# A transformer layer on one core: the lower left output quadrant is added on VectorE and stored plainly

## What is computed

```python
    mix = jnp.concatenate([attn_out, u], axis=-1) @ w_out[l]
    x = x + g1 * mix                                    # called x1 below
    h2 = modulate(rms_norm(x, norm_ffn_w[l]), sh2, sc2)
    up = depthwise_conv(h2 @ w_up[l], ffn_conv_w[l], ffn_conv_b[l])
    gate, val = jnp.split(up, 2, axis=-1)
    x = x + g2 * ((jax.nn.silu(gate) * val) @ w_down[l])   # (1024 x 2816) @ (2816 x 1024)
```

## Time and profile before

| | |
|---|---|
| median of 3 runs | 1184.42 us (1182.46 to 1187.9) |
| profiled execution | 1190.29 us, of which the span from the first to the last instruction is 1188.4 us |
| mean granted TensorE clock | 0.983 |
| busy share of the span | PE 95%, DVE 79%, ACT 49%, POOL 25% |
| DMA | 171.77 MB, 145 GB/s in the mean |

### The profile page before, as it was taken

The page is one execution under the profiler, slowest core; times in us unless marked ns, Lnnn a source line. Parts: engine busy times, 40 slices in busy tenths (PEclk is TensorE's granted clock), DMA queues, the critical chain, the costliest instruction groups (busy, mean ns, idle before and its releaser), DMA issues.

```text
span 1188.4 us, 17094 instructions
## 1 busy us (share of the span) xinstructions
PE 1128.5 (95%) x5953; PEld 959.4 (81%) x5953; DVE 937.2 (79%) x1422; ACT 577.2 (49%) x991; POOL 296.4 (25%) x337
## 2 busy tenths in 40 slices
PE   7899999899998999998799999999999999999995
PEld 7687888799888887876688888787888878888884
DVE  0579988779997754469999999999999966877763
ACT  1662356766556764455343434343443534444441
POOL 2200111135454000002555454545510020000111
PEclk9999999999998999999899999999999999999998
DMA  9422556529999315222545454545433284543574
GB/s 364 159 75 77 120 107 117 145 46 257 245 240 277 107 46 170 86 88 90 159 127 180 135 171 131 171 129 175 136 111 106 91 307 159 118 114 98 125 160 62
DMA packets 103090, 171.77 MB, mean 145 GB/s; under 512 B 9322, under 2 KB 62690, under 8 KB 102004
## 3 DMA queue, kind: packets, MB, share of 16 engines
q1 hardware_dynamic: 82388, 104.70, 26.7%
q0 software_dynamic: 20640, 66.27, 23.9%
HBM read 112.21 MB, written 31.46 MB: 121 GB/s over the span
## 4 chain that ended last, share of the span: by engine, by line
PE 37%; DVE 13%; issue 7%; ACT 5%; DVEq 0%; ACTq 0%; POOL 0%
PE ps L1684 14%; PE ps L1734 6%; PE ps L1736 6%; PE ps L1735 6%; PE ps L1649 5%; DVE y L2100 3%; DVE w_op L2001 3%; DVE w_raw L2019 2%; DVE y L2096 2%; ACT w_op L1805 2%; ACT y L1893 1%; DVE u L2089 1%; DVE s_sum L2019 1%; ACT h_second L1798 0%; PE ps L1660 0%
## 5 line engine op out<-in xcount | busy, mean ns | idle before, releaser
L1684 PE MATMUL ps<-t_op,w_op 128*128 128x512 f32 x1056 | 247.5, 390 | 2.5 <-issue 0.9
L1684 PEld LDWEIGHTS ps<-t_op,w_op 128*128 128x128 f32 x1056 | 197.9, 188 | 46.0 <-issue 2.9
L1684 PE MATMUL ps<-hx,w_op 128*128 128x512 f32 x792 | 192.0, 396 | 9.6 <-DVE u L2089 7.0
L1684 PEld LDWEIGHTS ps<-hx,w_op 128*128 128x128 f32 x792 | 151.0, 191 | 43.3 <-DVE u L2089 6.5
L1805 ACT ACTIVATE w_op<-w_raw 128x512 fp32r<-128x512 f32 x132 | 79.9, 623 | 193.8 <-DVE w_raw L2019 191.6
L1734 PE MATMUL ps<-dnh,ah 128*128 128x512 f32 x308 | 120.1, 390 | 1.6 <-DVE dnl L2107 1.6
L1735 PE MATMUL ps<-dnl,ah 128*128 128x512 f32 x308 | 119.8, 389 | 0.0
L1736 PE MATMUL ps<-dnh,al 128*128 128x512 f32 x308 | 119.8, 389 | 0.0
L2001 DVE TENSOR_TENSOR w_op<-w_raw,w_op 128x512 fp32r<-128x512 f32 x132 | 102.5, 791 | 9.8 <-ACT w_op L1805 7.7
L1913 ACT ACTIVATE ah<-hid 128x512 fp32r<-128x512 f32 x77 | 48.6, 631 | 116.8 <-PE ps L1736 112.8
L2107 DVE TENSOR_TENSOR al<-hid,ah 128x512 fp32r<-128x512 f32 x77 | 53.3, 692 | 48.8 <-ACT ah L1913 48.1
(11 more groups left out here) (293 smaller groups left out, 2392.2 us busy)
## 6 DMA issues: line engine op xcount, KB each, us to landing
w_raw<-in_w_up SPq DMA_DIRECT2D x44, 512.0 KB, 5.1
wm<-in_w_mod SPq DMA_DIRECT2D x32, 512.0 KB, 6.4
sums<-wm POOLq DMA_DIRECT2D x32, 512.0 KB, 8.1
wd<-in_w_down POOLq DMA_DIRECT2D x44, 256.0 KB, 3.4
w_down_sums<-wd POOLq DMA_DIRECT2D x44, 256.0 KB, 2.8
dn_raw<-w_down_sums SPq DMA_DIRECT2D x44, 256.0 KB, 2.6
hid_scratch<-hid SPq DMA_DIRECT2D x20, 512.0 KB, 4.4
hid<-hid_scratch POOLq DMA_DIRECT2D x20, 512.0 KB, 5.2
```

The lines of the kernel that those rows point to most:

```text
L1684: last = pe.matmul(bank_of(p, s), w_op[p][w][:, k, :], rows_of(p, k, v), start=(start and k == 0 and w == 0 and v == 0), stop=(k == KH - 1 ...
```

## The change

It touches only the lower left quadrant.

- GpSimd's 4 adding transfers of `w21` and 4 of `c21` are gone, with the wait between them. GpSimd's last wait is now for the 12 transfers that are left, of which those of c12 are the last.
- Before the load of step 49 (`BASE_STEP = (7, 5)`: product 7, pair 5) SP issues 4 loads of the lower left quadrant of x1 (256 KB each) from `out` into `p1_all`. Ahead of them it waits for the x1 stores and for the last `u2`.
- New quad operation `b21` behind each `c12`: VectorE adds `w21` to the loaded x1 in `p1_all`.
- At the end `c21` writes its product with the gate into `w21`, and a new quad operation `o21` adds it to `p1_all`: one more VectorE operation per row block.
- SP then waits for each `o21`, stores `p1_all` to `out` without adding (256 KB each, 4 of them), and waits for the four stores.

```diff
-        QUAD_OPS += [(name, t) for t in range(4) for name in ("s12", "c12")] + [("c21", t) for t in range(4)]
+        QUAD_OPS += [(name, t) for t in range(4) for name in ("s12", "c12", "b21")] + [(name, t) for t in range(4) for name in ("c21", "o21")]
+        BASE_STEP = (7, 5)
...
+            def lower_left(t):
+                return out[0, HALF + t * P:HALF + (t + 1) * P, 0:HALF]
...
                 for n in range(4, NSTEP):
+                    if n == step_of(*BASE_STEP):
+                        sp.wait_ge(x1_out, 16 * TT)
+                        sp.wait_ge(quad_read, quad_at("u2", 3))
+                        for t in range(TT // 2):
+                            sp.dma_start(p1_all[:, t, :], lower_left(t)).then_inc(base_in, 16)
                     load_step(n)
+                for t in range(TT // 2):
+                    sp.wait_ge(quad_read, quad_at("o21", t))
+                    sp.dma_start(lower_left(t), p1_all[:, t, :]).then_inc(x1_out, 16)
+                sp.wait_ge(x1_out, 16 * (TT + TT // 2))
...
+                    elif name == "b21":
+                        dve.wait_ge(base_in, 16 * (TT // 2))
+                        ins = dve.tensor_tensor(out=p1_all[:, t, :], in0=p1_all[:, t, :], in1=w21[:, t, :], op=ALU.add)
+                    elif name == "c21":
+                        dve.wait_ge(bank_mm, TT // 2 - 1 + t + 1)
+                        ins = dve.tensor_tensor(out=w21[:, t, :], in0=ps[:, t, :], in1=g2[0], op=ALU.mult)
                     else:
-                        dve.wait_ge(bank_mm, TT // 2 - 1 + t + 1)
-                        ins = dve.tensor_tensor(out=p1_all[:, t, :], in0=ps[:, t, :], in1=g2[0], op=ALU.mult)
+                        ins = dve.tensor_tensor(out=p1_all[:, t, :], in0=p1_all[:, t, :], in1=w21[:, t, :], op=ALU.add)
...
                 for t in range(TT // 2):
                     quad("c21", t)
+                    quad("o21", t)
...
-                    accumulate("c22", t, 1, 1, g22[:, t, :], stored)
-                    accumulate("w21", t, 1, 0, w21[:, t, :], w21_stored)
+                    accumulate("c22", t, 1, 1, g22[:, t, :])
                 for t in range(TT // 2):
-                    accumulate("c12", t, 0, 1, g12[:, t, :], stored)
-                pool.wait_ge(w21_stored, 16 * 4)
-                for t in range(TT // 2):
-                    accumulate("c21", t, 1, 0, p1_all[:, t, :], stored)
-                pool.wait_ge(stored, 16 * 16)
+                    accumulate("c12", t, 0, 1, g12[:, t, :])
+                pool.wait_ge(stored, 16 * 12)
```

More of the change, by code:

```diff
@@ L1501, in build @@
             back_in = [sem4(f"back_in{i}") for i in range(NXT)]
-            dn_sum, dn_hi, dn_split, dn_mm, bank_mm, p1_copied, quad_read, stored, w21_stored = (
-                sem4(n) for n in ("dn_sum", "dn_hi", "dn_split", "dn_mm", "bank_mm", "p1_copied", "quad_read", "stored", "w21_stored"))
+            dn_sum, dn_hi, dn_split, dn_mm, bank_mm, p1_copied, quad_read, stored, base_in = (
+                sem4(n) for n in ("dn_sum", "dn_hi", "dn_split", "dn_mm", "bank_mm", "p1_copied", "quad_read", "stored", "base_in"))
             block = s4.enter_context(nc.Block())
@@ L2227, in _ @@
                     if i in (1, 3, 5, 7):
-                        for name in {6: ("c11",), 5: ("u2",), 7: ("u4",), 3: ("s22", "c22", "w21"), 4: ("s12", "c12")}.get(p, ()):
+                        for name in {6: ("c11",), 5: ("u2",), 7: ("u4",), 3: ("s22", "c22", "w21"), 4: ("s12", "c12", "b21")}.get(p, ()):
                             quad(name, i // 2)
@@ L2274, in _, with accumulate @@
                     reload(i)
-                def accumulate(name, t, rows_half, cols_half, src, done):
+                def accumulate(name, t, rows_half, cols_half, src):
                     pool.wait_ge(quad_read, quad_at(name, t))
                     r0 = (rows_half * (TT // 2) + t) * P
-                    pool.dma_start(out[0, r0:r0 + P, cols_half * HALF:(cols_half + 1) * HALF], src, accum_op=ALU.add).then_inc(done, 16)
+                    pool.dma_start(out[0, r0:r0 + P, cols_half * HALF:(cols_half + 1) * HALF], src, accum_op=ALU.add).then_inc(stored, 16)
                 pool.wait_ge(x1_out, 16 * TT)
                 for t in range(TT // 2):
-                    accumulate("c11", t, 0, 0, g11[:, t, :], stored)
+                    accumulate("c11", t, 0, 0, g11[:, t, :])
                 for t in range(TT // 2):
-                    accumulate("c22", t, 1, 1, g22[:, t, :], stored)
-                    accumulate("w21", t, 1, 0, w21[:, t, :], w21_stored)
+                    accumulate("c22", t, 1, 1, g22[:, t, :])
                 for t in range(TT // 2):
-                    accumulate("c12", t, 0, 1, g12[:, t, :], stored)
-                pool.wait_ge(w21_stored, 16 * 4)
-                for t in range(TT // 2):
-                    accumulate("c21", t, 1, 0, p1_all[:, t, :], stored)
-                pool.wait_ge(stored, 16 * 16)
+                    accumulate("c12", t, 0, 1, g12[:, t, :])
+                pool.wait_ge(stored, 16 * 12)
 def rope_table(np):
```

## The result

The changed kernel takes 1178.91 us in the median of 12 runs (1174.95 to 1186.06), the kernel before beside it 1186.59 (1181.91 to 1193.35, 12 runs). The ratio is 0.9941 with a 95% interval of [0.9913, 0.9968]: 7.0 us faster. The prediction had 7.2 us (1177.2 from 1184.42).

A forecast was written before the change was run, and what follows sets the result against it. TensorE, busy 95% of the span, was taken as the bound, leaving mainly the end to gain: VectorE +0.95, issue -0.63, landing -3.0, DRAIN -4.5, together -7.2 us from 1184.42 to 1177.2 us; range 1173.5 to 1183.5.

The forecast's parts named there:

- What bounds: Whole kernel: TensorE is busy 95% of the span; other engines' savings show only where it stands still, chiefly the last 12.1 us.
- VectorE, +0.95: End of the kernel: the last VectorE operation ends 0.95 us later, 0.72 for o21 and 3 x 0.08 for the pace.
- the part of the pace: Last four row blocks: dependent c21 and o21 pairs take 1.44 us against 1.36 per row block, costing 3 x 0.08 us.
- VectorE to issue, -0.63: End of the kernel: SP issues the last store 0.03 us after VectorE, where GpSimd's adding transfer took 0.66.
- Landing, -3.0: Last store: SP's plain store lands in 2.6 us (bounds 2.5 to 3.6) instead of 5.6 for the adding transfer.
- The DRAIN, -4.5: Block end: GpSimd's DRAIN of 4.63 us is hidden under the last product's matmuls; SP's of 0.12 us comes last instead.
- The rival in which it stays last: Block end: GpSimd's DRAIN still ends last or SP gets a costly one; only -2.7 us, 1181.7 us; chance 0.08.
- The loads, no cost: Before step 49: four issues of 0.32 us fit between loads; step 49's data lands in 5 to 6 us, under 9.4.
- TensorE's second cover of 3.5 us: Step 49: after ScalarE takes the load, another 3.5 us of slack before TensorE starts the step.
- b21, no cost: Steps 67, 69, 71 and 73: four VectorE operations of 0.72 us behind c12 fit into slack and cost nothing.
- The rival of the slow landing: Last store: it lands no faster than the adding transfer, 5.6 us; sum -4.2 us, 1180.2 us; chance 0.11.

The follow-up runs named there:

- the unchained kernel: The changed kernel with c21 waiting for its matmuls and not for the o21 of the row block before; ratio to the kernel before 0.9950.
- with plain stores: The changed kernel with its four last stores, still without adding, issued by GpSimd instead of SP; ratio to the kernel before 0.9990.
- with w21 folded in: The kernel before without w21's four adding transfers; VectorE adds w21 to c21, GpSimd still adds the sum to the output; ratio 1.0008.
- with SP waiting: The kernel before with SP, not GpSimd, waiting for the 20 adding transfers; ratio to the kernel before 0.9984.

## Why the prediction was right, step by step

- **What bounds:** only the time after TensorE's last matmul could change. It held: TensorE's row is full before it in both kernels.
- **VectorE, +0.95:** measured +1.0. First c21 to the end of the last o21 is 5.77 us, before 4.77 (1172.33 to 1177.10). The pairs came at 1.45 to 1.46 us, as foreseen, and the unchained kernel confirms the part of the pace.
- **VectorE to issue, -0.63:** measured 0.66 to 0.03. GpSimd, however, did not need 0.66 everywhere: its last issue came 0.29 us after the last o21 both with plain stores (1175.55 to 1175.84) and with w21 folded in (1175.19 to 1175.48). Before and with SP waiting, its second and third issue also came 0.29 to 0.30 us after their c21, and only the last 0.67 and 0.68. So it is not the pace of 1.36 us alone. What the last one waited for isn't settled; some 0.3 to 0.4 of the 0.6 us are not the queue's as such.
- **Landing, -3.0:** the mis-sized term. It measured -3.6 (5.6 to 2.0). I took 2.6 from stores of twice the size and set the bound below at 2.5, the least in any row; both were too high for these stores. That all but 0.3 of these 3.6 us are the adding's, and not the queue's, is shown by 2.3 us for the plain store from GpSimd. The trace before pointed there already, in rows that the prediction did not use: GpSimd's 44 plain stores of 256 KB to `w_down_sums` (line 2254) landed in 2.6 us at least, 2.8 in the median and 7.1 at most.
- **The DRAIN, -4.5:** measured -4.63: 4.63 gone from the end and 0.007 us for SP's in its place, not 0.12. The rest, landing to DRAIN and DRAIN to the end of the span, stayed at 0.4 us. Putting the DRAIN back costs 5.1 us. The rival in which it stays last has fallen: it ended 6.5 us before the engines met. In both blocks of every run it ended behind the landing of its own queue's last transfer, however long that took. The one of 11.6 us, which the prediction left open as a bound, fits this: a landing of 9.0 us and 2.6 us more.
- **The loads, no cost:** each issue took 0.43 us in the median and not 0.32, so four took 1.8 of the 2.7 us between two steps, still without a delay to step 49's issue at 1078.92, which came on its step. Its landing: 5.3 us, foreseen 5 to 6. TensorE's second cover of 3.5 us measured 3.4, with four times the loads.
- **b21, no cost:** the four stand in VectorE's idle time; no matmul waited for a low part after them.

The sum of the measured terms is +1.0 - 0.63 - 3.6 - 4.6 = -7.9 us (rounded), as between the two profiles (16.1 to 8.2); the ratio's 7.0 us has it inside its interval (3.8 to 10.3 us). The forecast of 7.2 was too small by the landing's 0.6 us and the DRAIN's 0.1. That 7.2 lies so near the 7.0 of the times says little, as the interval is 6.5 us wide. The forecast time, 1177.2, is 1.7 us below the measured median, mainly because it was counted from a median of 3 runs of before that lay 2.2 us under the one of 12.

The rival of the slow landing, 5.6 us, is out by 2.0 us measured. The sentence of the Trainium skill that was cited with it ("DMA: Bandwidth & Descriptors", section "Issuing engines are not separate DMA queues") agrees with the runs all the same in what it says: between the two queues the same plain store differs by 0.3 us only. The other one, the DRAIN of about 12 ns on every engine ("VectorE: DVE Perf Modes", section "The DRAIN you can't avoid" of the Trainium skill), does not describe the DRAINs here: SP's took 7 or 124 ns, GpSimd's 4.6 to 8.9 us in the last block. The page speaks of boilerplate DRAINs from a program's preamble and postamble; whether it means those at the end of a block at all, no run here shows.

## What to carry to other kernels

Read past the end of the chain of waits: the rows of the block's end tell which sequencer arrives last. At each block's end here GpSimd's DRAIN was over 2.6 to 5.6 us after GpSimd's last transfer had landed, save in the kernel that made it wait for SP as well; it was on the path where that transfer was the last to land, and off it where the rest of the kernel went on for longer. So end a kernel like this one on the queue with the cheap end, and let the other finish its part early: in the changed kernel GpSimd's last transfer landed 12 us before the end. Moving the wait alone gave 1.5 us of 4.6. An adding transfer at the very end can be exchanged for an early load, one VectorE addition and a plain store. In the middle, beside a full TensorE row, taking adding transfers away was worth nothing.

## What was not expected of the hardware

- GpSimd's DRAIN with nothing in flight took 4634 ns before, 5124 ns in all five kernels with 12 transfers by GpSimd in the last part, and 5451 ns in both kernels with 16. With 20 it was 4634 again, so it isn't the count alone. What sets it is open.
- A plain store of 256 KB by SP, with nothing before it in flight, landed in 2.0 us, less than any load of the same size by line 1628 in the trace before (2.5 at least); the adding kind took 3.7 to 7.4 us there.
- SP's DRAIN took 7 ns where SP's last instruction was a wait for a landing, and 123 to 124 ns where it was the issue of a load.
